# Hybrid retention/convolution layer on one core: conditioning products as fp32r parts with convolution taps moved, and orders changed in merge, FFN, up to down and opening

## The reference

```python
mod = silu(c) @ ada_w + ada_b          # c and c_ctx; sh1, sc1, g1, sh2, sc2, g2 = split(mod, 6)
h = rms_norm(x, n1_pre) * (1 + sc1) + sh1
q, k, v, g_ret, u_a, u_b, gate_ret, gate_conv = split(h @ w_in)      # 1024 columns each
o = bidirectional_retention(rope(q), rope(k), v)                     # 4 heads, chunks of 128
ret_out = (silu(g_ret) * head_group_norm(o)) @ ret_w_out
u = depthwise_conv(u_a * sigmoid(u_b), width=31)
conv_out = silu(layer_norm(u)) @ conv_w_out
mixed = sigmoid(gate_ret) * ret_out + sigmoid(gate_conv) * conv_out
x = x + g1 * rms_norm(mixed @ w_mix_out, n1_post)
h2 = rms_norm(x, n2_pre) * (1 + sc2) + sh2
a, gl = split(depthwise_conv(h2 @ ffn_w_up, width=3))                # 2816 columns each
x = x + g2 * rms_norm((silu(a) * gl) @ ffn_w_down, n2_post)
```

## Time and profile before

| | us |
|---|---|
| median of 3 runs | 2181.98 (2180.94 to 2182.82) |
| the profiled execution | 2183.2 |
| its span, first to last instruction | 2180.4 |
| PE busy | 2132.1 (98%) |
| PE weight load busy | 1955.3 (90%) |
| DVE busy | 1607.5 (74%) |
| ACT busy | 783.6 (36%) |
| POOL busy | 967.1 (44%) |
| mean granted TensorE clock | 0.994 of full |

### The profile page before, as it was taken

One profiled execution on the slowest core, in us unless ns is written; L12 is line 12 of the kernel. 1 busy time (PEld: TensorE's weight loads), 2 busy tenths in 40 slices (PEclk: granted clock), 3 DMA queues, 4 the chain that ended last, 5 costly groups with the idle time before them and its releaser, 6 DMA issues.

```text
span 2180.4 us, 31469 instructions
## 1 busy us (share of the span) xinstructions
PE 2132.1 (98%) x12411; PEld 1955.3 (90%) x12411; DVE 1607.5 (74%) x1826; ACT 783.6 (36%) x1326; POOL 967.1 (44%) x619
## 2 busy tenths in 40 slices
PE   7999999999999999999999999999999999999998
PEld 3888988988988899999899988899999999978887
DVE  3689489489489477787536536699898988766775
ACT  3501101101101266665538233243343333434342
POOL 1323323323323366665382121146666656565563
PEclk9999999999999999999999999999999999999999
DMA  9442442442432455544554444212222323385653
GB/s 299 126 140 79 134 131 79 134 131 79 132 107 88 158 156 167 181 144 152 196 173 147 138 165 138 97 47 75 73 80 61 91 62 91 107 305 178 202 181 129
DMA packets 246594, 291.77 MB, mean 134 GB/s; under 512 B 12241, under 2 KB 198961, under 8 KB 246449
## 3 DMA queue, kind: packets, MB, share of 16 engines
q1 hardware_dynamic: 178401, 221.33, 32.0%
q10 hardware_dynamic: 66640, 63.72, 9.0%
q0 software_dynamic: 1408, 4.72, 0.6%
HBM read 222.71 MB, written 67.01 MB: 133 GB/s over the span
## 4 chain that ended last, share of the span: by engine, by line
PE 89%; DVE 4%; ACT 2%; SPq 1%; DMA 1%; issue 1%; POOL 1%; ACTq 0%; DVEq 0%; POOLq 0%
PE ps L956 87%; DVE f_cv L2567 1%; DVE T_raw L2527 1%; SPq L647 1%; PE ps L1166 1%; DMA x_all<-in_x_sample 1%; PE ps L1214 0%; POOL Wa_lo L1962 0%; DMA sh_row<-gain_d 0%; ACT sq_t L1453 0%; DVE x_all L2185 0%; DMA g_raw<-g_d 0%; PE ps L1007 0%; POOL f_cv L2105 0%; PE ps L1299 0%
## 5 line engine op out<-in xcount | busy, mean ns | idle before, releaser
L2242 DVE SCALAR_TENSOR_TENSOR conv_y<-u_in,VC,conv_y 128x1167 f32<-128x1167 f32 x240 | 396.0, 1650 | 7.4
L1962 POOL TENSOR_TENSOR Wa_lo<-W_raw,Wa_hi 128x1024 fp32r<-128x1024 f32 x58 | 143.8, 2486 | 392.3 <-ACT Wa_hi L1422 392.0
L956 PE MATMUL ps<-A_hi,Wa_hi 128*128 128x384 f32 x768 | 270.5, 352 | 1.4 <-ACT vg_st L1545 0.8
L956 PE MATMUL ps<-A_hi,Wa_lo 128*128 128x384 f32 x768 | 258.7, 337 | 0.0
L956 PE MATMUL ps<-A_lo,Wa_hi 128*128 128x384 f32 x768 | 258.5, 337 | 0.0
L2567 DVE SCALAR_TENSOR_TENSOR f_cv<-f_in,VF,f_cv 128x1023 f32<-128x1023 f32 (+1 forms) x176 | 216.5, 1281 | 3.6 <-ACT f_cv L1849 1.9
L1962 POOL TENSOR_TENSOR D_lo<-F_raw,D_hi 128x1024 fp32r<-128x1024 f32 x66 | 162.3, 2462 | 98.0 <-ACT D_hi L1422 98.0
L2604 DVE TENSOR_TENSOR g_lo<-g_raw,g_hi 128x384 fp32r<-128x384 f32 x66 | 139.4, 2121 | 78.7 <-ACT g_hi L1422 78.7
L2100 POOL TENSOR_TENSOR O_lo<-E,O_hi 128x512 fp32r<-128x512 f32 x80 | 130.1, 1626 | 151.5 <-ACT O_hi L1422 151.5
L956 PE MATMUL ps<-Wb_hi,A_hi 128*128 128x512 f32 x432 | 179.7, 416 | 0.0
L2100 POOL TENSOR_TENSOR O_lo<-F_raw,O_hi 128x512 fp32r<-128x512 f32 x68 | 113.1, 1666 | 146.3 <-ACT O_hi L1422 146.3
(11 more groups left out here) (286 smaller groups left out, 5563.9 us busy)
## 6 DMA issues: line engine op xcount, KB each, us to landing
F_raw<-in_ffn_w_down SPq DMA_DIRECT2D x66, 512.0 KB, 3.6
F_raw<-in_ffn_w_up SPq DMA_DIRECT2D x44, 512.0 KB, 6.1
qt<-qkvg_d SPq DMA_DIRECT2D x36, 512.0 KB, 3.8
W_raw<-in_w_in SPq DMA_DIRECT2D x32, 512.0 KB, 5.2
W_raw<-in_w_in SPq DMA_DIRECT2D x64, 256.0 KB, 3.2
ada_w<-in_ada_w ACTq DMA_DIRECT2D x30, 512.0 KB, 4.3
g_d<-f_cv SPq DMA_DIRECT2D x22, 576.0 KB, 3.6
g_raw<-g_d SPq DMA_DIRECT2D x66, 192.0 KB, 3.7
```

The source lines that it names most:

```text
L956: return pe.matmul(out, l, r, start=start, stop=stop)
L1962: return pool.tensor_tensor(dst, x, Fv(hi), ALU.subtract)
L2242: dve.scalar_tensor_tensor(out=y, in0=x, scalar=tap, in1=y, op0=ALU.mult, op1=ALU.add).then_inc(q.conv_step, 1)
```

## The change

The 4096 later columns of `ada_w` become 16 chunks of 256 columns, each in two halves of four k blocks: 32 pieces x. A piece is loaded, split (ACT writes `ada_h`, single-buffered; POOL writes `ada_l` in place over `ada_w`), and multiplied in 8 steps: the stationary operand is now `cs4` (128 x 4: hi and lo of the two conditionings), the moving one 256 columns of `ada_h` or `ada_l`, in fp32r. A finished chunk is a row block of 4 x 256, copied to `row_s`, turned by two transposes on PE and copied to `mod4`; DVE adds its hi and lo columns at the end. Piece 4i lies in group 2 of `u_tile(i, 0)`, the others in q tiles 1, 4, 7 (2, 4, 6, 8 for i = 0). Tap 0 of the long convolution goes from DVE to ACT (`conv_first`), and the last 8 taps of block 7 into the opening of the retention. Besides these there are changes of order in four places. Shortened to its core ("..." marks what is left out):

```diff
 # PE
             def ada_early(n):
-                pe.wait_ge(ada_in[n % 4], 16 * (n // 4 + 1))
+                if n == 0:
+                    pe.wait_ge(ada_half_in, 16)
                 for k in range(KT):
+                    if k == (4 if n == 0 else 0):
+                        pe.wait_ge(ada_in[n % 4], 16 * (n // 4 + 1))
...
+            def ada_rows_turn(ch):
+                pe.wait_ge(q.adaU_ok, 2 * ch + 1)
+                for m in range(2):
+                    last = pe.transpose(ps[:, 6 + ch % 2, 256 + 4 * m:260 + 4 * m], row_s[0:4, m * P:(m + 1) * P], ident[0:4, 0:4])
+                last.then_inc(q.ada_used, 1)
+            def ada_part(x, step):
+                k, part = divmod(step, 2)
+                if step == 0:
+                    if x % 2 == 0 and x >= 2:
+                        ada_rows_turn(x // 2 - 1)
+                    if x % 2 == 0 and x >= 4:
+                        pe.wait_ge(q.adaU_ok, x - 2)
+                    pe.wait_ge(q.ada_lo, x + 1)
+                w = ada_h[:, k, :] if part == 0 else ada_l[:, x % 2, k, :]
+                last = mm(ps[0:4, ada_bank(x), 0:256], cs4[:, x % 2 * 4 + k, :], w, x % 2 == step == 0, x % 2 == 1 and step == 7)
...
 # SP: start, opening, up to down
-            ada_chunk(0)
+            for ks, done in ((slice(0, 4), ada_half_in), (slice(4, 8), ada_in[0])):
+                sp.dma_start(ada_p[:, 0, ks, :], ada[:, ks, 0:2 * P]).then_inc(done, 16)
...
-            for b in (3, 4):
-                kv_load(b)
-            for s_ in conv_st:
-                sp.wait_ge(s_, 16 * KT)
-            for n in range(4):
-                tile_load(n)
-            s0f_load(0)
             for s in range(-NT, N_STEP):
                 b = piece(s)
-                if b is not None and 2 <= b < 32 - 3:
+                if s == -5:
+                    ...   # the same wait, the four tile loads, s0f_load(0)
+                if b is not None and b + 3 < 32:
                     kv_load(b + 3)
...
             down_raw(0)
             down_raw(1)
-            g_store(FKT - 2)
+            for c in range(4):
+                down_g(c)
             down_raw(2)
             down_raw(3)
-            for c in range(4):
-                down_g(c)
+            g_store(FKT - 2)
 # ACT
+            def ada_split(x):
+                if x:
+                    act.wait_ge(q.ada_used, ada_done(x - 1))
+                act.wait_ge(ada_in[x % 2], 16 * (2 + x // 2 + 1))
+                copy(ada_h[:, :, :], ada_w[:, x % 2, :, :]).then_inc(q.ada_hi, 1)
+            def ada_after(x):
+                if x + 1 < 32:
+                    ada_split(x + 1)
+                if x % 2 == 0 and x >= 2:
+                    ada_mods(x // 2 - 1)
+                if x % 2:
+                    ada_rows(x // 2)
+                if x + 2 < 32:
+                    ada_load(x + 2)
+            def conv_first(i):
+                act.wait_ge(q.u_ok, i + 1)
+                ...
+                act.activation(conv_y[:, i % 2, :], u_in[:, i % 2, 0:U_OUT], ACT.Identity, bias=..., scale=VC[:, i:i + 1]).then_inc(first_tap, 1)
             def q_out(i):
                 for t in range(NT):
+                    if t == 0:
+                        conv_first(i)
+                    if i == t == 0:
+                        ada_split(0)
+                    x = ada_q_piece(i, t)    # ada_after(x) before the rotated tile's store, or after the v/g tile's
...
-            for x in GATE_TAIL:
+            for x in GATE_TAIL[:-1]:
                 gate_out(x)
...
             for g in range(NTG):
                 hi_part(g, r_raw, r_hi, 0)
+                if g == 0:
+                    gate_out(GATE_TAIL[-1])
...
             op_hi(op_no(2, U_S2))
-            T_hi_part(T_4)
             for n in range(3, 6):
                 evac(1, n)
+            T_hi_part(T_4)
             op_hi(op_no(2, U_S3))
...
             centre_tap(FKT - 1, 0)
+            for c in (4, 5):
+                down_hi(c)
+                g_hi_part(c)
             silu(FKT - 1)
 # POOL
+            def ada_lo_part(x):
+                pool.wait_ge(q.ada_hi, x + 1)
+                sub(ada_l[:, x % 2, :, :], ada_w[:, x % 2, :, :], ada_h[:, :, :]).then_inc(q.ada_lo, 1)
             for i in range(KT):
...
+                if i:
+                    ada_lo_part(4 * i + 1)     # before u_in; the next ones behind conv_store and two lo_w
...
-            conv_store(KT - 1)
             lo_w(N_S1 + 2)
             for s in range(-NT, N_STEP):
...
+                if s == -6:
+                    conv_store(KT - 1)
...
-            for c in range(4):
+            for c in range(6):
                 down_lo(c)
             product(FKT - 1)
 # DVE
-                    taps_u(i, range(CW))
+                    taps_u(i, range(1, CW - LAST_TAPS if i == KT - 1 else CW))     # LAST_TAPS = 8
...
             value_b(0)
-            dve.wait_ge(q.adaU_ok, 4)
+            taps_u(KT - 1, range(CW - LAST_TAPS, CW - LAST_TAPS + 2))
+            dve.wait_ge(q.adaU_ok, 32)
+            then(dve.tensor_tensor(mod[:, 16:48, :], mod4[:, :, 0:2], mod4[:, :, 2:4], ALU.add))
...
+                if s + NT in range(LAST_TAPS // 2 - 1):      # two taps at each of s = -9, -8, -7
+                    w = CW - LAST_TAPS + 2 * (s + NT + 1)
+                    taps_u(KT - 1, range(w, w + 2))
```

More of the change, by code:

```diff
@@ L135, in build @@
         gm1 = kept("gm1", [P, 64])
+        gmr_at = kept.pieces[0][0]
         gmr = kept("gmr", [64, P])
+        mod4 = at("mod4", [P, 32, 4], gmr_at)
         kept_end = kept.pieces[0][0]
@@ L150, in build @@
         u_a = s1("u_a", [P, T])
-        ada_w = s1("ada_w", [P, 2, KT, P])
+        ada_w_at = s1.pieces[0][0]
+        ada_w = s1("ada_w", [P, 2, 4, 256])
+        ada_l = at("ada_l", [P, 2, 4, 256], ada_w_at, F32R)
         qk_st = s1("qk_st", [P, 3, 512])
@@ L155, in build @@
         rope = s1("rope", [P, 3, 2, 256])
+        ada_h = s1("ada_h", [P, 4, 256], F32R)
+        row_s = at("row_s", [4, 256], up32(end_at))
         s0 = Region((startup_at, a_at))
@@ L596, in build, with ada_q_piece, ada_bank, ada_done @@
         ON_ACT = lambda j: j < 2 * KT and j % KT % 3 == 1
-        def ada_unit_of(i, part):
-            return 4 * i + part - 1 if i or part == 3 else None
-        def ada_at(x):
-            return 6 + x // 8 % 2, 2 * (x % 8)
+        ADA_TILES = {i: (2, 4, 6, 8) if i == 0 else (1, 4, 7) for i in range(KT)}
+        def ada_q_piece(i, t):
+            at_ = ADA_TILES[i]
+            return 4 * (i + 1) - len(at_) + at_.index(t) if t in at_ else None
+        def ada_bank(x):
+            return 6 + x // 2 % 2
+        def ada_done(x):
+            return 16 + x + 1 + x // 2
+        def ada_turned(ch):
+            return 16 + 3 * (ch + 1)
+        def ada_src(x):
+            return ada[:, x % 2 * 4:x % 2 * 4 + 4, 2048 + x // 2 * 256:2048 + (x // 2 + 1) * 256]
         LN_MEAN, LN_VAR = {5: 0, 6: 1, 8: 2}, {11: 0, 13: 1, 15: 2}
@@ L719, in _ @@
             for x in range(2):
-                sp.dma_start(ada_w[:, x, :, :], ada[:, :, (16 + x) * P:(17 + x) * P]).then_inc(ada_in[x], 16)
+                sp.dma_start(ada_w[:, x, :, :], ada_src(x)).then_inc(ada_in[x], 16)
             for r in range(3):
@@ L1009, in _ @@
             pe.wait_ge(q.dk_exp, 1)
[L1010 to L1018 removed]
+            def ada_rows_turn(ch):
[13 more added lines that the diff above has]
+                last = mm(ps[0:4, ada_bank(x), 0:256], cs4[:, x % 2 * 4 + k, :], w, x % 2 == step == 0, x % 2 == 1 and step == 7)
+                if step == 7:
                     last.then_inc(q.ada_used, 1)
@@ L1057, in first_u @@
                             last.then_inc(q.u_ps, 1)
-            def ada_among(x, step, first, every):
-                if x is not None and step % every == first:
-                    ada_part(x, step // every)
             def u_tile(i, e):
@@ L1072, in u_tile @@
                                lambda k: A_hi[:, tiles, k, :], lambda k: A_lo[:, tiles, k, :],
-                               between=lambda k: ada_among(ada_unit_of(i, e), KT * g + k, 1, 3))
+                               between=lambda k: ada_part(4 * i, k) if e == 0 and g == NTG - 1 else None)
                 last.then_inc(q.u_ps, 1)
@@ L1547, in q_out @@
                             vg_store(h, t - 1)
+                        if x is not None:
+                            ada_after(x)
                 if g:
@@ L1942, in e_root @@
                 act.activation(est[:, n, 2:3], est[:, n, 1:2], ACT.Sqrt).then_inc(q.e_s, 1)
-            for c in range(4, N_CH):
+            for c in range(6, N_CH):
                 down_hi(c)
@@ L2558, in side_taps @@
                 n0 = tap_no(j, kind) - 4
[L2559 removed]
+                dve.wait_ge(q.fc0, KT + c0_no(j, kind))
                 for n in which:
```

102 lines of the change are left out of this document (54 added, 48 removed).

## The result

| | us |
|---|---|
| kernel before, median of 4 runs (one more than above) | 2182.40 (2180.94 to 2185.07) |
| changed kernel, median of 4 runs | 2163.65 (2163.26 to 2165.91) |
| ratio, 95% interval | 0.9911 (0.9899 to 0.9922) |
| profiled execution of the changed kernel, its span | 2165.9, 2164.1 |

Faster by 18.8 us, not by 31.9, and outside the range. First the page of the changed kernel: busy time by engine, the chain by engine, and one group (busy, mean ns | idle before).

A forecast was written before the change was run, and what follows sets the result against it. PE, 89% of the chain that ended last, was taken as the bound. Stage -21.0, opening +0.5, start 0, merge -3.4, FFN -4.0, up to down -4.0 made -31.9 us: 2150.1 us expected, range 2143 to 2162.

The forecast's parts named there:

- FFN: FFN block 2: evacuations moved ahead of `T_hi_part(T_4)` end PE's stop, POOL's `U_S3` part preceding the first `T_lo`; -4.0 us.
- Conditioning products: Projections: 256 fp32 products (59 us) become fp32r ones of 256 columns (30.7 us) plus transposes; net 25 us less on PE.
- The transposes: Conditioning: 16 x 2 small transposes added on PE, 0.22 us per group of two, 3.5 us (bounds 2.6 and 6.2).
- Rival D: Conditioning: products with a four-column stationary operand cost 0.23 us like the old pair; 2178 us, chance 0.03.
- First piece: q half 0, tile 2: PE waits once, some 4.3 us (bounds 0 and 5), as POOL is with two weight parts.
- DVE and the taps: Projections: POOL's 32 new parts cost DVE 35 to 80 us, 65 to 110 us stay idle; costed at nothing.
- Rival E: q halves: DVE becomes the bound, blocked taps using up the five tiles of lead; slower, 2200 us, chance 0.04.
- Rival A: FFN: the stop moves to `U_S3`, POOL blocked behind both `T_lo`; 2150.1 + 3.5 = 2153.6 us, chance 0.22.
- Merge: Merge start: eight `r_hi` before the last gate copy let PE start earlier; -3.4 us (bounds -1 and -4.5).
- Up to down: Between FFN up and down: earlier loads of g and reordered chunks 4 and 5 remove two stops; -4.0 us.
- Opening: Opening of the retention: moved taps, with `conv_store(7)` and loads about three steps later; +0.5 us (bounds -2 and +3).
- start: Start of the kernel: first `ada_w` chunk in halves, hidden by PE's wait for the third chunk; 0 (bounds -1 and +1).

The follow-up runs named there:

- experiment 3: Changed kernel with ACT's parts of `U_S3` and `U_A22` ahead of `T_hi_part(T_4)` in the FFN; 2161.88 us.
- experiment 7: Changed kernel without the four reorderings, POOL's 32 `ada_l` subtractions cut to 8 of 256 columns, PE multiplying `ada_h` in place of `ada_l`; 2160.99 us.
- experiment 6: Changed kernel with only the last eight taps put back in q half 7, the other edits kept; 2177.31 us.
- experiments 5: Changed kernel without its reorderings in opening, merge, FFN and up to down, the last eight taps back in q half 7; 2175.61 us.
- experiment 8: Changed kernel with the last gate copy after four `r_hi` instead of eight; 2162.28 us.
- experiment 9: Changed kernel with `g_lo` of chunk 4 ahead of the last taps on DVE and SP's block 21 store behind chunk 10's loads; 2162.41 us.
- experiment 10: Changed kernel with the first chunk of `ada_w` loaded whole, as in the kernel before; 2165.29 us.

## Why the prediction was wrong

The forecast missed by several terms. The largest is the FFN, where the step itself went the other way; with that term alone put right the forecast would be 2156.1 us, inside the range. One more error, in the taps, does not show in the sum, since a part of the change hid it.

- **Conditioning products: right in kind, the size a little off.** "256 fp32r products of 256 columns, which follow each other at 0.12 us": 0.12 us to the next start, but the 512-column products between two of them start 0.231 to 0.234 us apart instead of 0.227, so that one costs 0.138 us in a q tile (mean of 168; 200.04 to 200.86 is one) and 0.123 in a u tile. The transposes: a pair adds 0.30 us (from 199.51 to 200.04 lie 0.53 us, of which 0.23 are the product's), not 0.22. A round of u tiles and q half takes 78.97 us instead of 81.72. Rival D (narrow products dear) is out. Without the first stop and its slow products the stage is 15.7 + 7.0 = 22.7 us shorter, forecast 25; 200 x 0.138 + 56 x 0.123 + 16 x 0.30 = 39.3 us were added instead of 34.2, and so some 62 removed instead of 59.
- **First piece: place and cause right, 4.3 us against 7.** In the profiled execution the weights' DMAs landed later than before, and POOL started their parts at 97.86 instead of 95.43. In that of experiment 3 it started them at 95.59, and the stop was 4.27 us, the forecast's number. What had no term at all is the clock behind the stop, 1.6 us. The kernel before pays it too after its stops (11 products in the merge, 22 in the FFN), and my reading of its rows passed over it. The Trainium skill, "TensorE: Matmul & The Clock Gate", "Part 1: The HAM clock gate", says that TensorE's clock falls to 1.2 GHz for want of work and comes back under load; the distances of 0.43 and 0.23 us agree.
- **DVE and the taps: the term that carried the gain was costed at nothing.** I bounded the contention by 35 to 80 us; DVE's two groups grew by 87 us on the 240 taps (482.7 us in all against 396.0) and 24 on `qk_st` (54.8 against 31.0), 3.5 us for each new part; experiment 7 shows 85 of these 111 us to hang on the width of the new parts. The error of method is the balance: idle time summed over a stage covers nothing at its end, where DVE had less than 1 us. Without the moved taps the kernel would be 6 us faster than before instead of 19 (experiment 6). I had a term neither for the stop nor for what holds it off, and that the two errors cancel in my sum is luck. Rival E has the cause right and the place wrong: inside the q halves the five tiles of lead held (PE's table of waits from 88 to 703 us has the first piece alone), but they don't cover the last taps of block 7, which stand ahead of `vb_lo`.
- **FFN: the failed step, 6 us.** "PE wants it after the 48 products of `U_S2`": a product is 24 matmuls, 3.2 us, so PE was there at 1433.4 and not 3 us later. And "it gets in ahead of them": POOL's record began first, yet both `T_lo` went before it. The edit cost 2.0 us instead of winning 4.0. Rival A was the true case, and dearer than its 3.5 us: in the kernel before the 24 products of `U_S2` ran from 1450.67 to 1456.71 at the low clock, while POOL's part ended at 1456.56, so the slow products had hidden the same delay.
- **Merge: right.** -2.9 us instead of -3.4; the slow products stay. All the runs without the new place of the gate copy (the kernel before, experiments 5 and 7) stop 5.0 us there, those with it 1.9 to 2.5, or 0.9 with experiment 8's.
- **Up to down: half right.** The first stop is gone, the second split into 0.89 and 1.01 us: -2.1 instead of -4.0. "The 2.42 us stop has no cause left" overlooked DVE, where `g_lo(4)` stands behind eight taps, and SP, where later loads stand behind the store of block 21 (experiment 9, which changed both, takes the two stops away; it doesn't say how much each had).
- **Opening: +1.3 us instead of +0.5 in the profiled execution, start 0 as forecast** (+1.3 in the profiled execution, but see experiment 10). From the gates to the first product with `T_hl` PE needs 47.7 us in the kernel before and 49.0 in the changed one. In the other eight profiled executions with the changed opening it needs 47.0 to 49.6, and 47.0 to 47.1 in the three where no slow products follow the wait for `vb_lo`. So the opening's cost can't be told from what the low clock does there.

Against the forecast that makes 2.3 (products), 2.7 (first piece), 6.0 (FFN), 1.9 (up to down), 0.5 (merge) and 0.8 (opening): 14.2 us, where 13.1 are missing by the medians. The stages are those of one execution each, so the rest of 1.1 us means nothing.

## What to carry to other kernels

Count an engine's slack where the next stage begins, not over the stage: an instruction that blocks another engine's is paid at the first point where the two have to meet. An edit that moves a wait is worth little where the engine behind the wait is full (here 2.8 of 8.5 us); look at its busy time in that stretch before reordering around it. Price a TensorE stop with the slow products behind it, and try the parts of a change singly: here one part made a stop that another hid.
